# A two-layer encoder on one core: the four norm stages dissolved into their neighbours, and the products of a recurrence reordered

## What is computed

```
h   = x * rsqrt(mean(x*x) + 1e-6) * g * (1 + scale(c)) + shift(c)
x  += gate(c) * sublayer(h)
```

## Time and profile before

| | |
|---|---|
| median of 3 runs | 4754.56 us |
| profiled execution | 4747.91 us |
| its span, first to last instruction | 4746.1 us |
| TensorE busy, matmuls | 4508.4 us (95%) |
| VectorE / ScalarE / GpSimd busy | 2374.5 / 1484.2 / 305.6 us |
| granted TensorE clock, mean | 0.977 of full |

### The profile page before, as it was taken

One profiled execution on the slowest core, in us unless ns is written; L12 is line 12 of the kernel. 1 busy time (PEld: TensorE's weight loads), 2 busy tenths in 40 slices (PEclk: granted clock), 3 DMA queues, 4 the chain that ended last, 5 costly groups with the idle time before them and its releaser, 6 DMA issues. The chain is left out here.

```text
span 4746.1 us, 64348 instructions
## 1 busy us (share of the span) xinstructions
PE 4508.4 (95%) x24356; PEld 3607.4 (76%) x24356; DVE 2374.5 (50%) x4003; ACT 1484.2 (31%) x2082; POOL 305.6 (6%) x167
## 2 busy tenths in 40 slices
PE   6997999999999999989599999879999999999999
PEld 3464888888888888834499999848888888888887
DVE  5764885553245555430354555338855532444444
ACT  2252333333222222211343333223333332222222
POOL 0001340000000000001200000013400000000000
PEclk9998999999999999989799999999999999999999
DMA  6302245656566666433300000023455665555553
GB/s 235 139 1 71 93 143 188 205 202 209 172 224 232 230 217 235 154 109 106 126 27 25 19 24 19 25 83 97 138 191 203 208 203 177 186 199 199 180 196 132
DMA packets 248143, 690.92 MB, mean 146 GB/s; under 512 B 12920, under 2 KB 78712, under 8 KB 239904
## 3 DMA queue, kind: packets, MB, share of 16 engines
q1 hardware_dynamic: 240544, 654.99, 40.7%
q0 software_dynamic: 7424, 33.56, 1.9%
HBM read 533.27 MB, written 155.22 MB: 145 GB/s over the span
## 5 line engine op out<-in xcount | busy, mean ns | idle before, releaser
L1321 DVE TENSOR_TENSOR pe_lo<-pe_raw,pe_hi 128x2048 fp32r<-128x2048 f32 x222 | 508.9, 2292 | 1265.5 <-ACT pe_hi L1101 1265.5
L796 PE MATMUL bank<-pe_hh,pe_hi 128*128 128x512 f32 x2304 | 913.4, 396 | 51.4 <-POOL pe_lo L1199 49.1
L798 PE MATMUL bank<-pe_hh,pe_lo 128*128 128x512 f32 x2304 | 899.7, 390 | 0.0
L797 PE MATMUL bank<-pe_hl,pe_hi 128*128 128x512 f32 x2304 | 899.2, 390 | 0.0
L796 PE MATMUL bank<-pe_ah,pe_hi 128*128 128x512 f32 x2048 | 796.7, 389 | 0.0
L797 PE MATMUL bank<-pe_al,pe_hi 128*128 128x512 f32 x2048 | 796.7, 389 | 0.0
L798 PE MATMUL bank<-pe_ah,pe_lo 128*128 128x512 f32 x2048 | 796.7, 389 | 0.0
L1101 ACT ACTIVATE pe_hi<-pe_raw 128x2048 fp32r<-128x2048 f32 x272 | 520.5, 1913 | 588.2 <-PE bank L798 580.1
L796 PEld LDWEIGHTS bank<-pe_hh,pe_hi 128*128 128x128 f32 x2304 | 433.6, 188 | 140.9 <-POOL pe_lo L1199 51.0
L798 PEld LDWEIGHTS bank<-pe_hh,pe_lo 128*128 128x128 f32 x2304 | 433.3, 188 | 91.2
L797 PEld LDWEIGHTS bank<-pe_hl,pe_hi 128*128 128x128 f32 x2304 | 434.1, 188 | 85.5
(11 more groups left out here) (272 smaller groups left out, 5096.4 us busy)
## 6 DMA issues: line engine op xcount, KB each, us to landing
pe_raw<-in_stream SPq DMA_DIRECT2D x272, 1024.0 KB, 5.7
acts<-h SPq DMA_DIRECT2D x128, 512.0 KB, 7.1
gates<-pe_stage SPq DMA_DIRECT2D x32, 2048.0 KB, 7.4
pe_w<-gates SPq DMA_DIRECT2D x32, 2048.0 KB, 10.2
h<-acts SPq DMA_DIRECT2D x128, 512.0 KB, 4.1
ada_ring<-in_ada_w SPq DMA_DIRECT2D x32, 768.0 KB, 6.5
at_ada_ring<-in_ada_w POOLq DMA_DIRECT2D x16, 1024.0 KB, 6.6
rwkv_proj<-rp_out POOLq DMA_DIRECT2D x64, 256.0 KB, 2.7
```

The costliest lines, as they stand in the source:

```text
L796: nc.tensor.matmul(out, left[0], right[0], start=start, stop=False)
L797: nc.tensor.matmul(out, left[0], right[1], start=False, stop=False)
L798: return nc.tensor.matmul(out, left[1], right[0], start=False, stop=stop)
L1321: nc.vector.tensor_tensor(lo[:, side], raw[:, side], hi[:, side].bitcast(F32), ALU.subtract).then_inc(low, 1)
```

## The change

Two edits. First, `stage_norm` is gone. The squares, the mean, the root and the reciprocal stand at the tail of the stage ahead, and write the reciprocal to a tile `K.rstd` that outlives the stage. The scaling and the shift stand at the head of the stage behind.

```
+def square_rows(K, act, norm, c, square):
+    K.nc.scalar.activation(square(c), K.x[:, c, :], ACT.Square).then_inc(norm.squared, 1)
+def mean_of_squares(K, pe, norm, bank, square):
+    for c in range(DC):
+        pe.wait_ge(norm.squared, c + 1)
+        last = K.nc.tensor.matmul(K.ps[bank][:, :], K.const("ones_d"), square(c), start=(c == 0), stop=(c == DC - 1))
+def root_of_mean(K, act, norm, bank, out):     # PSUM to PSUM
+    K.nc.scalar.activation(K.ps[out][:, :], K.ps[bank][:, :], ACT.Sqrt, bias=K.eps[:, 0:1])
+def invert_root(K, dve, norm, root):
+    K.nc.vector.reciprocal(K.rstd[:, :], K.ps[root][:, :]).then_inc(norm.inverted, 1)
```

```
+                    act.wait_ge(scaled, c + 1)
+                    nc.scalar.activation(hh[:, c, :], K.hc(c), ACT.Identity, bias=shift_of(K, layer, 1, c)).then_inc(h_high, 1)
...
+                for c in range(DC + 1):
+                    if c < DC:
+                        scale_rows(K, layer, 1, c, scaled)
+                    if c >= 1:
+                        dve.wait_ge(h_high, c)
+                        nc.vector.scalar_tensor_tensor(out=hl[:, c - 1, :], in0=K.hc(c - 1), scalar=shift_of(K, layer, 1, c - 1),
+                                                       in1=hh[:, c - 1, :].bitcast(F32), op0=ALU.add, op1=ALU.subtract)
```

Second, in `rwkv_mix` the products and banks are reordered, as are the waits of TensorE (VectorE and ScalarE follow the same order):

```
-        KINDS = ("N", "NT", 0, 1, 2)
-        BANKS = {(kind, z): 2 * ((5 * z + i) % 4) for z in range(2) for i, kind in enumerate(KINDS)}
+        KINDS = (("N", 0), ("NT", 0), ("N", 1), ("NT", 1)) + tuple((i, z) for z in range(2) for i in range(3))
+        BANKS = {kind: 2 * (i % 4) for i, kind in enumerate(KINDS)}
+        TOK_BANKS = (2, 3, 6, 4, 5)
+        P_BANK, Q_BANK, T_BANK, SUM_BANK = 4, 0, 6, 2
...
-                    if not first:
-                        pe.wait_ge(y_out, 8 * c)
+                    for i, src in enumerate((B[:, side, 0], B[:, side, 1], intail[:, side, 0], C[:, side, 0], C[:, side, 1])):
+                        if i == 3 and not first:
+                            pe.wait_ge(y_out, 8 * c)
...
+                    pe.wait_ge(tok_out, 5 * c + 3)
+                    products("N", 1, A, B, side, n_done, (tok_out, 5 * c + 4))
+                    products("NT", 1, B, A, side, nt_done)
+                    products(0, 0, C, A, side, masked_done, (prod_out, made + 1))
+                    products(1, 0, B, R, side, masked_done, (nt_out, 4 * c + 1))
+                    products(2, 0, C, R, side, masked_done, (prod_out, made + 3))
+                    products(0, 1, C, A, side, masked_done, (nt_out, 4 * c + 3))
+                    products(1, 1, B, R, side, masked_done, (prod_out, made + 5))
+                    products(2, 1, C, R, side, masked_done, (prod_out, made + 7))
-                    pe.wait_ge(prod_out, 16 * c + 16)
-                    pe.wait_ge(nt_out, 4 * c + 4)
```

More of the change, by code:

```diff
@@ L262, in _ @@
                 sum_modulation(K, acc, summed, n=EARLY // P)
[L265 to L307, removed]
@@ new lines, in _, with __init__ @@
+                mean_of_squares(K, pe, norm, 1, K.hc)
+class NormSems:
+    def __init__(self, K, tag):
+        self.squared = K.sem(tag + "_squared")
+        self.meaned = K.sem(tag + "_meaned")
+        self.deviated = K.sem(tag + "_deviated")
+        self.inverted = K.sem(tag + "_inverted")
+def square_rows(K, act, norm, c, square):
+    K.nc.scalar.activation(square(c), K.x[:, c, :], ACT.Square).then_inc(norm.squared, 1)
+def mean_of_squares(K, pe, norm, bank, square):
+    for c in range(DC):
+        pe.wait_ge(norm.squared, c + 1)
+        last = K.nc.tensor.matmul(K.ps[bank][:, :], K.const("ones_d"), square(c), start=(c == 0), stop=(c == DC - 1))
+    last.then_inc(norm.meaned, 1)
@@ L310, in stage_output, with shift_of, shift_rows @@
+def shift_of(K, layer, sub, c):
+    return K.mod[:, layer, 24 * sub + c:24 * sub + c + 1]
+def shift_rows(K, act, layer, sub, scaled, shifted):
+    for c in range(DC):
+        act.wait_ge(scaled, c + 1)
+        K.nc.scalar.activation(K.hc(c), K.hc(c), ACT.Identity, bias=shift_of(K, layer, sub, c)).then_inc(shifted, 1)
 def stage_output(K):
@@ L484, in _ @@
             def _(dve):
+                for c in range(DC):
+                    scale_rows(K, 0, 0, c, scaled)
                 for half in range(2):
@@ L706, in stage_attention @@
         added = K.sem("at_added")
+        norm = NormSems(K, "n01")
         with nc.Block() as block:
@@ L724, in _ @@
                                          bias=K.eps[:, 0:1]).then_inc(sub_std, 1)
+                for c in range(DC):
+                    act.wait_ge(added, c + 1)
+                    square_rows(K, act, norm, c, K.hc)
+                root_of_mean(K, act, norm, 7, 0)
             @block.vector
@@ L1191, in _ @@
                 down_bodies(act, down)
+                if with_ada:
+                    for c in range(DC):
+                        act.wait_ge(added, c + 1)
+                        square_rows(K, act, norm, c, K.hc)
+                    root_of_mean(K, act, norm, 0, 1)
             @block.gpsimd
@@ L1444, in _ @@
                                                    op0=ALU.mult, op1=ALU.add).then_inc(added, 1)
+                invert_root(K, dve, norm, 6)
+            @block.scalar
+            def _(act):
+                for c in range(DC):
+                    act.wait_ge(added, c + 1)
+                    square_rows(K, act, norm, c, square)
+                root_of_mean(K, act, norm, 7, 6)
             @block.tensor
@@ L1455, in _, with rwkv_project @@
                     last.then_inc(projected, 1)
-def rwkv_project(K):
+                mean_of_squares(K, pe, norm, 7, square)
+def rwkv_project(K, ada_acc):
     nc, io = K.nc, K.io
@@ L1509, in _ @@
                 for c in range(DC):
+                    scale_rows(K, 1, 0, c, scaled)
+                for c in range(DC):
+                    dve.wait_ge(h_ready, c + 1)
                     nc.vector.tensor_tensor(xx[:, c, :], K.h[:, c, 0:T], K.h[:, c, 2:T + 2], ALU.add).then_inc(shifted, 1)
@@ L1902, in body @@
                                                       ).then_inc(prod_out, 1)
+                    for z in range(2):
                         for i in range(3):
@@ L2118, in body @@
                         double_p(lv, 1)
-                        if lv == 2 and not first:
-                            transpose_y(c - 1)
+                        if lv == 2:
+                            pe.wait_ge(prod_out, made + 16)
+                            if not first:
+                                transpose_y(c - 1)
                         double_q(lv, 0)
@@ L2204, in build @@
         K.end_stage()
-        stages = (("norm00", lambda: stage_norm(K, 0, 0)), ("attn", lambda: stage_attention(K)),
-                  ("norm01", lambda: stage_norm(K, 0, 1)), ("peer0", lambda: stage_peer(K, 0)),
-                  ("norm10", lambda: stage_norm(K, 1, 0)), ("rwkv", lambda: stage_rwkv(K)),
-                  ("norm11", lambda: stage_norm(K, 1, 1)), ("peer1", lambda: stage_peer(K, 1)))
-        for name, stage in stages:
-            if only is None or name in only:
-                stage()
-                K.end_stage()
+        with ExitStack() as across:
+            stage_attention(K)
+            K.end_stage()
+            shared = K.sb(across, "pe_shared", [P, TC, HP, NK])
+            stage_peer(K, 0, shared)
+            K.end_stage()
+            rwkv_project(K, modulation_sums(shared))
+        stage_rwkv(K)
+        K.end_stage()
+        with ExitStack() as across:
+            stage_peer(K, 1, K.sb(across, "pe_shared1", [P, TC, HP, NK]))
+            K.end_stage()
         stage_output(K)
```

116 lines of the change are left out of this document (74 added, 42 removed).

## The result

| | before | after |
|---|---|---|
| median of 4 runs each, us | 4753.93 | 4667.85 |
| lowest to highest | 4748.93 to 4756.17 | 4666.62 to 4669.28 |
| profiled execution, us | 4747.91 | 4669.28 |
| its span, us | 4746.1 | 4667.2 |
| granted clock, mean | 0.977 | 0.982 |

The changed kernel takes 0.982 of the time before [0.9803, 0.9837], 86.1 us less, against a forecast of 4670. The two profiled executions differ by only 78.6 us, and their spans by 78.9.

What follows compares the result with a forecast made beforehand. TensorE was taken as the bound, so only its waits pay, while norm stages run one engine at a time. Norms 45.4, order 22.4, y 2.5 and clock 14.0 sum to 84.3 us: 4754.6 to 4670, range 4656 to 4698.

Steps and rivals of the forecast that it cites:

- boundary 1: Modulation to attention: attention starts at 47.5 instead of 55.52, with the mean kept at 9.07 us; gain 8.0 us.
- boundary 2 with its head: Attention to peer 0: mean 7.1 us, stage starts at 420.75 instead of 431.19, gain 10.4 us; peer head 0.5 more.
- boundary 3: Peer 0 to RWKV: stage starts at 2026.2 instead of 2048.70, less scalings in the head; net gain 17.1 us.
- boundary 4 with its head: RWKV to peer 1: stage starts at 3149.4 against 3158.33, gain 8.9 us; peer head 0.5 more.
- recurrence: order, y, clock: Recurrence: earlier level 1 saves 22.4 us, transposes ahead of y 2.5, fewer half-clock stretches behind the wait 14.0.
- inside the other stages: Rest of the stages: no term in the forecast's sum; a peer stage changing by over 3 us would be wrong.
- the 64 hidden passes: RWKV head: 64 passes of the other modulation columns take 10 us at half clock, hidden in 16.0 before the first projection.
- A: Rival, recurrence: half clock comes from the small products, not the wait, so the 14 us stay; 4684 us, chance 0.13.
- B: Rival, peer heads: each operation there costs 2 us, 7 us more per head; 4684 us, chance 0.08.
- C: Rival, recurrence: VectorE bounds the reordered products, the wait moves on, order, y and clock gains go; 4709 us, chance 0.10.
- D: Rival, peer stages: tiles moved by pe_shared read slower, 8 ns a pass making the kernel 4774 us; chance 0.02.
- I take that as constant: Whole kernel: the median's 6.7 us above the profiled execution stays the same after the change.

Runs made afterwards that it cites:

- e5: Changed kernel with the mean ahead of the 32 one-column passes at peer 0's tail, and the reciprocal ahead of finish_modulation; 4662.59 us, ratio 0.9813 to the kernel before.
- e3: Kernel before, with TensorE multiplying constants into a free bank during its wait ahead of level 1; 4734.37 us, ratio 0.9968.
- e1: Kernel before with only the new rwkv_mix (recurrence) of the changed kernel, norm stages kept; 4710.8 us, ratio 0.9918.
- e4: Changed kernel, but level 1 again waits for all 16 masked copies; 4717.05 us, ratio 0.9931 to the kernel before.
- e11: The changed kernel run again without edits, in a later group; 4667.91 us, ratio 0.9823 to the kernel before.
- e10: Kernel before, with products of constants filling only 1.3 us of TensorE's 2.5 us wait ahead of level 1; 4742.3 us, ratio 0.9981.
- e2: Changed kernel with the old rwkv_mix (recurrence) of the kernel before, new norms kept; 4706.34 us, ratio 0.9907 to the kernel before.
- e6: Changed kernel, with VectorE instead of GpSimd making the first low part of each peer stage; 4664.53 us, ratio 0.9819 to the kernel before.
- e7: Changed kernel, with the recurrence's 8 chunks written out instead of a loop over 6; 4657.82 us, ratio 0.9804 to the kernel before.

## Why the prediction was right

| step | predicted | profiled executions |
|---|---|---|
| boundary 1 | 8.0 | 7.65 |
| boundary 2 with its head | 10.9 | 11.5 |
| boundary 3 | 17.1 | 15.5 |
| boundary 4 with its head | 9.4 | 9.4 |
| recurrence: order, y, clock | 38.9 | 38.7 |
| inside the other stages | 0 | -3.8 |
| sum | 84.3 | 78.9 |

**Boundaries 1, 2 and 4.** The forecast chain, mean, root, reciprocal, stage start, is what the timelines show, and the stage behind starts its loads where it was said, 0.1 and 0.2 us later in boundaries 2 and 4 and 0.8 later in boundary 1 (48.34 instead of 47.5). There the sums of the modulation were 0.5 late, and the mean, which stayed slow as forecast, took 9.51, above the upper bound of 9.07 (8.8 to 9.8 in the eight later profiles with this tail). That the weights landed 0.5 us sooner behind the stage's start than before gave part of it back. Taking 7.1 for the mean in the two others was right (7.04, 7.03). The heads gave 1.2 us rather than 0.5 in boundary 2.

**Boundary 3 was over-estimated by 1.6 us.** "The 32 passes left take 2.9": 3.55. "I take 8.0" for the mean: 8.75, the upper bound of the forecast. From the end of the mean to the stage's first issue 5.1 instead of 4.8. The head gave 0.1 back (15.9, not 16.0). The mean's slowness is shown by e5 to follow from the passes in front of it. The step behind the first of these is a row misread: "11 passes per us" counts all passes that touch the microsecond, and the prediction's own row has 23 passes in 2.62 us, which makes 3.6 for 32. The same error hit the 64 hidden passes, "10 us": at half clock each takes 0.213 us, twice the 0.111 of the first 32, in sum 13.8. That the projection still waited for VectorE saved the term.

**Recurrence.** The three terms can be read apart. First transposes to level 1: 21.7 us over 8 chunks (22.4). The y wait: the recurrence part went from 21.14 to 20.59 in five chunks, 2.75 (2.5). Levels: 14.2 (14.0). The cause given for the last, the wait and not the small products, is shown by e3 and by e1.

**The rivals.** A fell with e3. B: single `hl` take 0.74 and the heads gained. C: VectorE's last copy ends 0.7 us later than before, and still no wait moves on, since level 1 begins with nine of the sixteen copies; e4 shows what it costs if it needs all. D: the pace is 397 ns a pass against 396 in the up half and 389 against 389 in the down half, and peer 1 takes 1552.89 against 1552.91 us from its second copy out to the start of its last pass. The 1 ns in the up half goes with the fall at 544.0 in peer 0; the moved tiles cost nothing that peer 1 shows.

**What was missed and cancelled.** "Inside stages: 0" was wrong by 3.8. Attention is 1.4 us longer and peer 0 1.8, and in each TensorE fell to half clock at a place where it had not in the profiled execution before, at 199.2 us and at 544.0. In the profile of e11 neither fall is there, so this varies from run to run. But the change has a part in the second: the wait of TensorE ahead of it was 1.76 us long and is 2.11 in every profile with the new norms and the old head of the up half. In those the clock fell behind it in 5 of 7; behind waits of 1.76 at this place of either peer stage it fell in 2 of 15. Why the wait grew isn't shown. Its row in the kernel before, counterpart of the one at 543.61 above:

```profile
560.98 0.50 PE L796 MATMUL bank<-pe_hh,pe_hi 128*128 128x512 f32 x1 [1.76 <-POOL pe_lo L1199]
```

Another 0.8 us lies between the end of the recurrence and the end of its output projection, unexplained, and 0.2 came back ahead of the recurrence. "I take that as constant", the 6.7 us between the profiled execution and the median, failed. Before's profiled execution lay below all four runs of its group, and low among runs that reach from 4738.98 to 4758.79 over all groups; after's was the highest of its four. By the profiled executions (78.6) the forecast gained 5.7 us too much, by the medians 1.8 too little. That the median came within 2.2 us of 4670 owes something to the two misses having opposite signs.

**The spread, and what stays open.** Over all groups the kernel before spreads over 20 us in 36 runs, the kernel after over 3 in 9. The mean granted clock of each run goes with its time: of the kernel before's 32 runs beside the experiments, those at 0.975 take 4754.4 us on average, those at 0.976 4751.0, those at 0.977 4746.5; one of 4758.2 us has 0.974, and the fastest, 4738.98, has 0.979. So its spread is one of the clock. Much of it goes with the wait ahead of level 1: e3, which fills the wait, spreads over 4.0 us in 7 runs, where the kernel before beside it spreads over 16.2 in 10; e10, which fills half, spreads over 11.6 in 10. Which falls come and go between the kernel before's runs isn't shown, since only one of its executions was profiled. Nor is it shown why one wait of 2.5 us is followed by a fall and another isn't.

## What to carry to other kernels

A short chain of one engine at a time between two stages can be laid into the tail of one and the head of the next: price it by the chain that is left (mean 7.0, root 0.7, reciprocal 3.4), and look at the first instruction of the next stage that TensorE needs, since work moved into a head is free only up to that. Where TensorE waits one to three microseconds inside dense work, count the slower passes behind the wait as well, and split one wait for all results into waits for the results that each product reads. Take the offset between a profiled execution and the median for what it is, one draw from the spread of the runs, and put the granted clock of the runs beside their times before you look for another cause.

## What the runs showed of the hardware

- The wait ahead of level 1 against falls to half clock in the levels behind it, of eight chunks: no idle wait, 0 but for loop ends (after, e1, e3); 1.0 us, 2 (e10), both near other idle time; 2.5 us, 7 (before) and 6 (e2, with the same recurrence); 3.2 us, 8, and longer ones (e4). A chunk pays 1.6 us or a multiple near it: 54.47, then 56.11, 57.75, 59.37.
- A stretch of one-column passes keeps TensorE busy in the record, and the products behind it are slow: 8.75 against 7.04 for the same 16 passes. The one-column passes themselves take 0.111 us each at a granted clock of 1.0 (the 32 of the kernel after) and 0.213 at 0.5 (the 64, 13.79 us in the kernel after and in e5).
- An `hl` of VectorE that arrives while GpSimd makes a low part is held until just behind its end (4.48 against 0.74); with GpSimd idle the longest is 0.753 (e6).
- A loop's end costs TensorE 2.8 us of waiting for issue, twice in eight chunks, and a fall of the clock behind each; written out, both go (e7, 8.7 us).
